# The front of an S5 mixer rebuilt: three scaled B sets, split angle tables, parameters transposed first, two C sets ahead of the input

## The reference, cut to what matters

```python
shift1, scale1, gate1, ... = split(silu(c) @ ada_w[0] + ada_b[0], 6)
h = rms_norm(x, norm1_g[0]) * (1 + scale1) + shift1
# s5_mixer: 64 groups of 16 channels, 64 complex states each
dt = exp(log_dt)[:, None]
ab = exp(lam_re * dt) * (cos(lam_im * dt) + i sin(lam_im * dt))
f  = (ab - 1) / lam
bb = f[..., None] * (b_re + i b_im)
s_t = ab * s_{t-1} + bb u_t               # u = h, per group
y_t = Re(c s_t) + d_skip * h_t
g = gelu(y); mix = g * sigmoid(g @ w_glu + b_glu); x = x + gate1 * mix
```

## Time and profile before

| | us |
|---|---|
| median of 3 runs (lowest, highest) | 1293.61 (1289.32, 1295.51) |
| profiled execution, its own time | 1292.06 |
| its span, first to last instruction | 1290.3 |
| busy: PE / DVE / ACT / POOL | 1246.6 / 857.1 / 604.6 / 50.2 |
| mean granted TensorE clock | 0.984 |
| share of the chain that ended last: PE / DVE / ACT / DMA | 87% / 7% / 2% / 2% |

### The profile page before, as it was taken

How to read it: one execution, slowest core, us unless ns; L and a number is a source line. 1 busy time by engine, 2 the same in 40 slices (tenths; PEclk the granted TensorE clock), 3 DMA queues, 4 the chain that set the end, 5 groups by cost and what they waited for, 6 DMA issues and landing times.

```text
span 1290.3 us, 25331 instructions
## 1 busy us (share of the span) xinstructions
PE 1246.6 (97%) x10936; PEld 1164.3 (90%) x10936; DVE 857.1 (66%) x1173; ACT 604.6 (47%) x781; POOL 50.2 (4%) x67
## 2 busy tenths in 40 slices
PE   5989999999999999999999999999999999999997
PEld 4667899999966489999999999999998999999997
DVE  6999678886537776768456655447459666666443
ACT  5845633433335565543445434336334545544342
POOL 5300000000000000000000000000000000000000
PEclk8969999999999999999999999999999999999998
DMA  9965478987652928655565554455455434655452
GB/s 262 315 217 174 163 258 299 326 293 256 209 180 96 295 86 278 217 173 165 165 208 177 178 180 147 156 186 161 134 164 160 135 131 131 202 189 194 143 177 74
DMA packets 219705, 247.03 MB, mean 191 GB/s; under 512 B 5872, under 2 KB 209088, under 8 KB 219616
## 3 DMA queue, kind: packets, MB, share of 16 engines
q1 hardware_dynamic: 211616, 218.63, 52.2%
q0 software_dynamic: 7648, 26.86, 6.1%
q10 hardware_dynamic: 352, 0.23, 0.1%
HBM read 244.66 MB, written 1.05 MB: 190 GB/s over the span
## 4 chain that ended last, share of the span: by engine, by line
PE 87%; DVE 7%; ACT 2%; DMA 2%; issue 1%; ACTq 0%; DVEq 0%
PE PS L1746 86%; ACT PARTS L592 1%; DVE ARENA L1154 1%; DMA RING<-in_ada_w 0%; DMA H<-in_s_log_dt 0%; DMA RING<-in_mla_w_uq 0%; DVE X L1158 0%; DMA RING<-in_w_in 0%; DVE ARENA L1262 0%; DVE PARTS L1012 0%; PE PS L2375 0%; DVE ARENA L1324 0%; DVE WL L1034 0%; DVE ARENA L1265 0%; DVE SQ L995 0%
## 5 line engine op out<-in xcount | busy, mean ns | idle before, releaser
L1746 PE MATMUL PS<-PARTS 128*128 128x256 f32 (+3 forms) x3608 | 839.8, 283 | 0.0
L1746 PEld LDWEIGHTS PS<-PARTS 128*128 128x128 f32 (+1 forms) x3608 | 619.3, 189 | 1.4 <-issue 0.9
L1034 DVE TENSOR_TENSOR WL<-RING,PARTS 128x2048 fp32r<-128x2048 f32 (+2 forms) x189 | 387.3, 2053 | 236.3 <-ACT PARTS L592 236.1
L1746 PE MATMUL PS<-HH,WL 128*128 128x256 f32 (+3 forms) x1832 | 520.9, 284 | 1.9 <-DVE PARTS L1003 0.9
L1746 PE MATMUL PS<-HH,PARTS 128*128 128x256 f32 (+3 forms) x1832 | 518.6, 283 | 0.0
L592 ACT CAST PARTS<-RING 128x2048 fp32r<-128x2048 f32 (+2 forms) x189 | 324.0, 1716 | 290.9 <-DMA RING<-in_w_ffn_out 66.8
L1746 PEld LDWEIGHTS PS<-HH,WL 128*128 128x128 f32 (+1 forms) x1832 | 345.1, 188 | 7.8 <-issue 4.9
L1746 PEld LDWEIGHTS PS<-HH,PARTS 128*128 128x128 f32 (+1 forms) x1832 | 344.4, 188 | 0.4
L1746 PE MATMUL PS<-PARTS,WL 128*128 128x256 f32 (+1 forms) x832 | 236.9, 285 | 0.8 <-DVE PARTS L1645 0.5
L1746 PEld LDWEIGHTS PS<-PARTS,WL 128*128 128x128 f32 x832 | 158.1, 190 | 2.7 <-issue 1.8
L1746 PE MATMUL PS<-ARENA 128*32 128x63 f32 (+8 forms) x864 | 59.2, 272 | 4.3 <-issue 3.1
(11 more groups left out here) (348 smaller groups left out, 992.8 us busy)
## 6 DMA issues: line engine op xcount, KB each, us to landing
RING<-in_w_ffn_in SPq DMA_DIRECT2D x44, 1024.0 KB, 5.1
RING<-in_ada_w SPq DMA_DIRECT2D x32, 1024.0 KB, 8.6
RING<-in_ffn_w_gate SPq DMA_DIRECT2D x22, 1024.0 KB, 5.3
RING<-in_ffn_w_up SPq DMA_DIRECT2D x22, 1024.0 KB, 5.2
RING<-in_w_in SPq DMA_DIRECT2D x20, 1024.0 KB, 5.2
ARENA<-in_ada_w POOLq DMA_DIRECT2D x16, 1024.0 KB, 7.3
RING<-in_ffn_w_down SPq DMA_DIRECT2D x16, 768.0 KB, 4.5
RING<-in_w_ffn_out SPq DMA_DIRECT2D x16, 768.0 KB, 4.2
```

Of the source, the lines that this page charges most:

```text
L1034: V.tensor_tensor(WL[:, u % SLOTS, 0:w], RING[:, u % SLOTS, 0:w], WH[:, u % SLOTS, 0:w].bitcast(fp32), SUB)\
L1746: return nc.tensor.matmul(o, lhsT, rhs, start=start, stop=stop)
```

## The change

- Parameters: lam_re, lam_im and the step are transposed first (three transposes, ahead of X), and all the arithmetic is done on 128 partitions by 32. ScalarE's loads are issued in another order; its `Silu` and the squares change places with the sines and the copies of X.
- B: the output of a chunk's last step is taken from the state at the chunk's end, so the state takes B times powers 0 to 3: plain B is expanded once and serves both the first set and the taps. Three sets are scaled. The taps are three instead of four; D becomes a product of its own (`SKIP`), without the identity products.
- Tables: angle of step = coarse part + fine part, each on 256 elements per partition, added once over 2048.
- `c_set(0)` and `(1)` stand ahead of the vectors and the norm, `(2)` and `(3)` between the norm and the first products.
- TensorE: `ada_rows(4)` stands behind `b_u(0..3)`; `stat(0)` ahead of the meta tokens; `bt_of(0)` ahead of `ada_rows(1)`.
- SP: the late constants go ahead of unit 8 instead of unit 2. VectorE waits for them only ahead of the GLU's weights.

The diff, cut to its core:

```diff
-                if u == 2:
+                if u == 8:
                     sp.dma_start(CN[:, C_LATE:], A["consts"][:, C_LATE:]).then_inc(S["late_loaded"], 16)
...
+            act.wait_ge(S["lrow_dve"], 1)
+            nc.scalar.activation(LAM[:, 0, :], LT[:, 3, :], ACT.Exp).then_inc(S["lrow_act"], 1)
+            nc.scalar.preload_act_table_set("trig_and_small")
+            for b in range(2):
+                act.wait_ge(S["xt_ready"], b + 1)
+                nc.scalar.copy(X[:, 2 * b:2 * b + 2, NMETA:], ...).then_inc(S["res_ready"], 2)
+            act.wait_ge(S["lrow_dve"], 2)
+            nc.scalar.activation(LT[:, 13, :], LT[:, 6, :], ACT.Sin).then_inc(S["lrow_act"], 1)
...
+            b_blocks(0)
+            meta_copy()
+            b_blocks(1)
             c_compact()
-            b_blocks(0)
             row_copy(0)
...
+            b_blocks(3)
+            bt_out(2)
+            row_copy(3)
             std(0)
...
+            bt_out(3)
             nc.scalar.preload_act_table_set("trig_and_small")
...
             shift(0, ADA_SHIFT1)
-            b_blocks(None)
...
+            for k in range(1, CHUNK):
+                b_set(k)
...
+            for g, steps_of in enumerate((coarse, fine)):
+                V.tensor_tensor(part[3 * g], steps_of, turn, MUL)
+                V.tensor_tensor(part[3 * g + 1], steps_of, low_part, MUL)
+                ins = V.tensor_tensor(part[3 * g + 2], steps_of, high_part, MUL)
+            link(ins)
+            link(V.tensor_scalar(TURNS[:, 0:4:3, :], TURNS[:, 0:4:3, :], MAGIC, MAGIC, ADD, SUB))
+            link(V.tensor_tensor(TURNS[:, 2:6:3, :], TURNS[:, 2:6:3, :], TURNS[:, 0:4:3, :], SUB))
+            link(V.tensor_tensor(TURNS[:, 2:6:3, :], TURNS[:, 2:6:3, :], TURNS[:, 1:5:3, :], ADD))
...
+            link(V.tensor_scalar(m, f, MAGIC, MAGIC, ADD, SUB))
+            link(V.tensor_tensor(f, f, m, SUB))
+            V.tensor_scalar(m.bitcast(i32), f.bitcast(i32), 0x7FFFFFFF, None, ALU.bitwise_and)...
...
+            for k in range(2):
+                c_set(k)
             dve.wait_ge(S["tr_ready"], 1)
-            dve.wait_ge(S["late_loaded"], 16)
...
             scaled(0, GS[:, 0, :], H, "norm_scaled")
-            V.scalar_tensor_tensor(m, f, -1.0, f, MUL, ALU.max).then_inc(S["turn_cos"], 1)
...
-            for k in range(2):
+            for k in range(2, 4):
                 c_set(k)
...
             for kt in range(4):
                 turned_in(kt)
-            c_set(2)
-            c_set(3)
...
-            ada_rows(4)
             for kt in range(4):
                 b_u(kt)
+            ada_rows(4)
             ada_rows(5)
             ada_rows(6)
             for kt in range(4, KT):
                 b_u(kt)
```

More of the change, by code:

```diff
@@ L182, in build @@
         POW, at = arena(at, 2 * CHUNK, PAIRS)
+        CSETS = [t[:, 2 * i:2 * i + 2, :, :] for t in (CSET_EARLY, CSET_LATE) for i in range(2)]
         WPOW, at = arena(at, 2 * CHUNK, PAIRS)
@@ new lines, in _ @@
+            act.wait_ge(S["lrow_dve"], 2)
+            nc.scalar.activation(LT[:, 13, :], LT[:, 6, :], ACT.Sin).then_inc(S["lrow_act"], 1)
+            nc.scalar.activation(LT[:, 14, :], LT[:, 7, :], ACT.Sin, scale=-1.0, bias=hpi).then_inc(S["lrow_act"], 1)
+            act.dma_start(BF[:, :], A["b_forget_2"].rearrange("a h -> h a")).then_inc(S["bf_loaded"], 16)
+            for b in range(2, 4):
+                act.wait_ge(S["xt_ready"], b + 1)
+                nc.scalar.copy(X[:, 2 * b:2 * b + 2, NMETA:], PS[:, b, :].rearrange("p (m t) -> p m t", m=2)).then_inc(S["res_ready"], 2)
@@ L665, in _ @@
+            squares(0)
             act.wait_ge(S["cact_ready"], 1)
@@ L737, in k_out @@
                         rows = slice(32 * q, 32 * q + 32)
-                        ins = nc.scalar.copy(KWD[rows, 4 * b:4 * b + 4, :, rows], KTAPS[rows, 4 * b:4 * b + 4, :, :])
+                        ins = nc.scalar.copy(KWD[rows, 4 * b:4 * b + 4, 1:, rows], KTAPS[rows, 4 * b:4 * b + 4, :, :])
                     ins.then_inc(S["k_used"], 1)
@@ L1161, in post @@
                 posts[0] += 1
[L1164 to L1198, removed]
             def modulation(c0, c1, raw=None):
@@ L1235, in _, with turned_pairs, by_q @@
-            V.tensor_tensor(R4[:, 0, :], R4[:, 1, :], R4[:, 1, :], MUL)
-            link(V.tensor_tensor(power(0, 1), PTMP[:, 0, 0:PAIRS], PTMP[:, 1, 0:PAIRS], SUB))
+            def turned_pairs(t):
+                return t.rearrange("p (k q) -> p q k", q=4)
+            def by_q(r):
+                return LAM[:, r, :].rearrange("p (q k) -> p q k", q=4)
+            dve.wait_ge(S["lam_ready"], 1)
+            V.tensor_copy(LT[:, 0:3, :], PS[:, 6, 0:3 * PAIRS].rearrange("p (r k) -> p r k", k=PAIRS)).then_inc(S["lam_used"], 1)
@@ new lines, in _, with by_channel @@
+            V.tensor_tensor(LAM[:, 3, :], LAM[:, 1, :], LAM[:, 2, :], SUB)
+            V.reciprocal(L[8], L[8])
+            dve.wait_ge(S["lrow_act"], 4)
+            V.tensor_tensor(power(0, 0), LAM[:, 0, :], L[14], MUL)
+            V.tensor_tensor(R4[:, 1, :], LAM[:, 0, :], LAM[:, 0, :], MUL)
+            link(V.tensor_tensor(power(1, 0), LAM[:, 0, :], L[13], MUL))
+            def by_channel(table, i, k):
+                return table[:, i * CHUNK + k, :].unsqueeze(1).unsqueeze(3).broadcast_to([P, 2, PAIRS, GCH])
@@ L1252, in _ @@
+            V.tensor_tensor(L[18], L[18], L[19], SUB)
+            link(times(POW, 1, 1, POW, (power(0, 0), power(1, 0)), 2))
+            V.tensor_tensor(WPOW[:, 0, :], L[16], L[8], MUL)
+            link(V.tensor_tensor(WPOW[:, CHUNK, :], L[18], L[8], MUL))
             link(times(WPOW, 0, 3, POW, (WPOW[:, 0, :], WPOW[:, CHUNK, :]), 1))
[L1254 to L1255 removed]
             dve.wait_ge(S["b_loaded"], 32)
[L1258 to L1267 removed]
@@ L2045, in _ @@
             nc.tensor.transpose(PS[:, 4, 0:KT], CROW[:, :], ident[0:KT, 0:KT]).then_inc(S["cact_ready"], 1)
+            pe.wait_ge(S["lrow_act"], 1)
+            for r in range(3):
+                ins = nc.tensor.transpose(PS[:, 6, r * PAIRS:(r + 1) * PAIRS], LROW[0:PAIRS, r, :], ident[0:PAIRS, 0:PAIRS])
+            ins.then_inc(S["lam_ready"], 1)
             pe.wait_ge(S["x_loaded"], 16)
@@ L2052, in _ @@
                     ins.then_inc(S["xt_ready"], 1)
[L2053 to L2056 removed]
+            stat(0)
             pe.wait_ge(S["meta_loaded"], 16)
@@ L2070, in _ @@
             ada_rows(0)
-            stat(0)
-            ada_cols(0)
-            ada_rows(1)
             def bt_of(k):
@@ L2088, in _ @@
             bt_of(0)
+            ada_rows(1)
+            ada_cols(0)
+            bt_of(1)
             pe.wait_ge(S["vrow_loaded"], 16 * (len(VROWS) + 4))
@@ L2093, in _ @@
             ins.then_inc(S["tr_ready"], 1)
-            for k in range(1, 3):
-                ada_cols(k)
-                ada_rows(k + 1)
-                bt_of(k)
+            ada_rows(2)
+            ada_cols(1)
+            bt_of(2)
+            ada_rows(3)
+            ada_cols(2)
             ada_cols(3)
```

218 lines of the change are left out of this document (106 added, 112 removed).

## The result

The median over 8 runs is 1299.16 us (1296.12 to 1303.34), beside 1292.77 for the kernel before (8 runs on the same chip): 1.0049 of it, with a 95% interval of 1.0031 to 1.0067. That is 6.4 us: the interval lies above 1, so the changed kernel is slower, by about the 0.5% that the prediction took as the least difference that can be told. The time lies in the predicted range and 5 us above the forecast. The profiled execution took 1299.81 us, span 1298.0, mean granted clock 0.978; before it was 1292.06, 1290.3 and 0.984.

A forecast was written before the change was run, and what follows sets the result against it. VectorE bounds the chain to 69.61 us, then TensorE, whose queue decides. The input's 2.5 us gain is given back by the moved `ada_rows(4)`: `y_of(0)` at 96.0 against 95.41, +0.6 us, giving 1294.2 us; range 1285 to 1303.

The forecast's parts named there:

- one `b_u` group at 13.93: TensorE: `b_u(0..3)` at the 1.2 GHz clock, 13.93 us, and `b_u(4..7)` at 7.72; one group slow, chance 0.45.
- the gap ahead of `b_u(0)`: TensorE between `bt_of(3)` and the first `b_u`: 2.75 us idle for ScalarE's copy, table load and shift, costing the clock.
- the ring wait ahead of `ada_rows(6)`: TensorE: some 6 us of waiting for ring units 12 and 13, issued after `ada_rows(4)` at 68.4 and landed at 76.6.
- the parameters: VectorE's front: narrower parameter work from 9.3 on, first B set at 17.0 instead of 21.75, bounds 15.5 to 21.75.
- return within `b_u(0..3)`: Rival in the first `b_u` group: the clock comes back by itself, a restart costing 2.1 us; 1290.1 us, chance 0.08.
- the clock returns with `ada_rows(6)`: TensorE ahead of the second group: `ada_rows(6)` brings 2.4 GHz back, so `b_u(4..7)` takes 7.72 us, to 88.3.
- the slower rival: Both `b_u` groups at the low clock, shown by 1.2 GHz as `b_u(4)` starts: +9, 1302.6 us, chance 0.22.
- the end of `bt_of(3)`: TensorE ahead of the input: at 47.8 instead of 50.8, with unit 7 2.0 us sooner and about 1.0 less work.
- 2.5 us are won at this point: At the first `b_u`: input ready at 50.5, where the first `b_u` began at 53.05 before.
- the y stage: TensorE from `y_of(0)` to the GLU: taken as busy throughout, with as many `y_of` products and columns as before.
- The move's cost: `ada_rows(4)` behind `b_u(0..3)`: a 2.75 us gap with the low-clock price, 13.93, and later issue of units 12 and 13.
- both groups at 2.4 GHz: Faster rival: the 2.75 us of idle do not cost the clock, `y_of(0)` at 88.0; -7.5, 1286.1 us, chance 0.25.

The follow-up runs named there:

- e5: The kernel before with one move alone, `ada_rows(4)` behind `b_u(0..3)`: 1302.02 us, 1.0062 of the time before.
- e12: The changed kernel with 63 calls of a narrow, unread product early on TensorE, ahead of `ada_rows(2)`: 1308.16 us, 1.0132.
- e2: The changed kernel with four unread products filling the gap between `bt_of(3)` and `b_u(0)`: 1296.09 us, 1.0029.
- e1: The changed kernel with `ada_rows(4)` put back ahead of `b_u(0..3)`: 1291.73 us, 0.9998 of the time before.
- e3: The changed kernel with `ada_rows(6)` moved behind `b_u(4..7)`: 1301.25 us, 1.0053.
- e6: e1 plus five filler calls on the identity between `ada_rows(6)` and `b_u(4..7)`: 1292.2 us, 0.9991.
- e7: e6 with ScalarE's sine table load moved behind the first shift: 1290.53 us, 0.9982.
- e13: e7 without the filler products ahead of the second `b_u` group: 1291.67 us, 0.9995.
- e10: The kernel before with twelve filler products on the identity between `ada_rows(6)` and `b_u(4..7)`: 1291.25 us, 0.9985.
- e11: e7 with 63 calls of a narrow, unread product early on TensorE, ahead of `ada_rows(2)`: 1300.09 us, 1.005.
- e8: e6 with all four C sets behind the norm: 1293.71 us, 0.9997.

## Why the prediction came out as it did

**Right.** The order of the chain behind 54 us was as predicted, down to its prices: one `b_u` group at 13.93 with the clock at 0.50, the gap ahead of `b_u(0)` (2.92, predicted 2.75), the ring wait ahead of `ada_rows(6)` (6.70, predicted about 6), the clock back soon behind it, `b_u(4..7)` at 8.02. From `b_u(0)` to `y_of(0)` I had 45.5 us (50.5 to 96.0); it took 45.67. VectorE's steps came as summed: tables 11.7 (11.6), two C sets 7.3 (7.4), and the parameters 1.2 us sooner than put: their first step began at 7.93, not 9.3. It ended well ahead of the last `y_of`. The clock did not return within `b_u(0..3)`: by the rule of the Trainium skill that activity releases the throttle ("TensorE: Matmul & The Clock Gate", "What's actually happening") it should have, and the runs with a group of 13.8 to 13.9 us disagree with it as the row of before did.

**Luck in it.** Two of these hits are worth less than they look. The 45.67 is a sum of two misses: `b_u(4..7)` began 28.6 us behind `b_u(0)` instead of 30.1, and `y_of(0)` came 17.1 behind that instead of 15.4, with an idle piece of 1.14 in `ada_rows(7)`. And I had taken it that the clock returns with `ada_rows(6)`. It was still at 0.50 when `b_u(4)` started, which was my own sign for the slower rival, and came back within the next 1.3 us. In e5 and e12 the group behind the same wait was fast too (8.08, 8.10); in e2 it was not (13.93). So which of the two groups' prices is paid there is not explained.

**Wrong.** The prediction has "the first `h` is ready at 50.5" and "2.5 us are won at this point". That `h` came at 54.06, and 1 us was lost. The step that failed is the end of `bt_of(3)`, put at 47.8 with the durations of before. It ended at 51.2: unit 7's step began 0.7 later than put, the two `ada_cols` took 2.76 and `bt_of(3)` 3.65, because the clock fell at 46. I had priced the clock for the gap behind `bt_of(3)` and not for the waits and the 128x1 products ahead of it. How much of this is in every run is not settled: in the profiled execution of e1 `bt_of(3)` took 3.65 too, in those of e2, e3, e6, e7 and e13, where TensorE has the same order up to there, 1.94 or 1.95. In e2 the first `b_u` began at 51.97, in e3 at 53.62. So even without the fall 2.5 us were too many.

The second miss is the y stage, which I took as unchanged. From `y_of(0)` to the GLU it took 28.1 us instead of 25.6; `ada_rows(9)`, 16 products, took 7.0 us with an idle piece of 2.46 and the low clock behind it. The prediction calls TensorE busy from `y_of(0)` to the GLU. That was a misreading: the chain of before has two such pieces there, in other places, while `ada_rows(9)` was whole (1.90 us).

```profile
97.34 1.63 issue
...
113.14 1.43 issue
```

So it was not more idle time that came, but the clock that one piece now cost (10 products in 3.54 us). I did not see that these pieces move when products are added or moved.

**The sum again.** At the first GLU product the forecast was +0.6; with 3.6 for the input that came at 54.06 and not at 50.5, 0.2 between `b_u(0)` and `y_of(0)` and 2.5 in the y stage it is +6.9, what the trace shows. So the forecast, no change beyond the 0.5% bound, held by a hair (1.0049): two terms were short, and nothing in the prediction kept them within it. The move's cost itself is confirmed by e1 and e5, and that the shorter front earns nothing that can be told here by e1, which has all of it and ties with the kernel before. Of the rivals, both groups at 2.4 GHz came up whole in no run: at best one and a half are (e6, e7), and in the kernel before with a filler all but 25 products (e10). In that rival's sum 84.1 should be 83.8; nothing hangs on it.

## What to carry to other kernels

A shorter front pays only if the step that starts the next stage waits for it; look which wait ends last after the change, here a ring load, TensorE's queue and a table load, and not VectorE. On TensorE a moved step costs its new gap and the loads that its end releases, and both belong in the sum with the clock's price of the work behind them (13.9 us instead of 7.7). Filling one gap gave no clear gain here as long as the next one took the clock.

## What the runs showed of the hardware

The clock fell behind idle pieces as short as 1.55 us (ahead of `b_u(0..3)` in e5), 1.63 (e1) and 1.55 inside a group (e6). It also fell in a busy TensorE, in the 128x1 products at 46 us of the changed kernel. Yet it held over the 2.77 us of idle in e7. The windows of TensorE in e5, then in e7, show both:

```profile
51.00:52.50 1.50, 0.00 (x0) 1.00 1.10 347
52.50:53.50 1.00, 0.98 (x32) 1.00 1.11 349
53.50:54.50 1.00, 1.00 (x32) 0.61 1.06 330
```

```profile
48.90:51.60 2.70, 0.00 (x0) 1.00 1.10 348
...
53.50:61.60 8.10, 7.80 (x260) 1.00 0.99 316
```

So the length of one idle piece, by which I priced the gap ahead of `b_u(0)`, does not decide alone whether the clock falls. What the level hangs on besides is open.

Up to the GLU, TensorE stood for up to 3.27 us (e11) at counts of products some 126 to 128 apart or a multiple of that, not at each of them, with an instruction packet of 16.3 KB starting 2 to 3 us ahead of the end of each stop. Such a stop can cost the clock as well: 133 products took 7.04 us behind one in e6, 123 took 3.96 ahead of it.

Single runs scatter more in some of these kernels than before: e5 from 1291.5 to 1307.5, e8 from 1283.6 to 1300.5, with the same instructions each time. Part of that can lie behind the change: from the first GLU product to the end, where these kernels run the same products, the profiled executions took from 1168.2 us (e13) to 1176.0 (e10), and 1169.3 before. A few us won ahead of the GLU can be lost in that.
